# Attention with sinks: the sink logit as one more column of the scores, written by a product of the identity

## The reference, cut to what matters

```python
s_win = jnp.where(ok, s_win, NEG)
s_sink = jnp.broadcast_to(sink.reshape(1, 1, G, R, 1, 1), s_ctx.shape[:-1] + (1,))
w = jax.nn.softmax(jnp.concatenate([s_win, s_ctx, s_sink], axis=-1), axis=-1)
o = einsum(w[..., :K3], vw) + einsum(w[..., K3:K3 + L], v_c)
```

## Time and profile before

| what | value |
| --- | --- |
| median of 3 runs | 1803.98 us (1803.07 to 1807.21) |
| the profiled execution | 1804.19 us, of which the span shown in the profile is 1802.2 us |
| granted TensorE clock, mean | 0.983 of full speed |
| group B of layer 0, first maximum | at 357.4 us from the start of the span |
| group B of layer 1, last maximum | at 1355.2 us |

### The profile page before, as it was taken

The page is one execution under the profiler, slowest core; times in us unless marked ns, Lnnn a source line. Parts: engine busy times, 40 slices in busy tenths (PEclk is TensorE's granted clock), DMA queues, the critical chain, the costliest instruction groups (busy, mean ns, idle before and its releaser), DMA issues. The chain is left out here.

```text
span 1802.2 us, 28988 instructions
## 1 busy us (share of the span) xinstructions
PE 1681.4 (93%) x11814; PEld 1489.5 (83%) x11814; DVE 1176.8 (65%) x1676; ACT 823.4 (46%) x1244; POOL 271.1 (15%) x212
## 2 busy tenths in 40 slices
PE   6999999989898999999999989899898989999998
PEld 4778897768778999899999869769677778989897
DVE  5374737677348797886987965653767484747472
ACT  5433326646227534535435463232655283527161
POOL 0243632301200000000000023362311200000000
PEclk9999999999999999999999999999999999999999
DMA  9541112200346348258276023122300355546251
GB/s 384 167 155 56 51 48 91 86 1 2 139 149 270 132 175 315 95 207 317 70 283 241 23 101 131 71 84 99 135 2 1 117 195 226 202 149 249 102 187 47
DMA packets 45456, 250.27 MB, mean 139 GB/s; under 512 B 5998, under 2 KB 7452, under 8 KB 26652
## 3 DMA queue, kind: packets, MB, share of 16 engines
q1 hardware_dynamic: 43420, 245.49, 36.9%
q10 hardware_dynamic: 1920, 3.15, 0.5%
HBM read 218.73 MB, written 26.74 MB: 136 GB/s over the span
## 5 line engine op out<-in xcount | busy, mean ns | idle before, releaser
L880 POOL TENSOR_TENSOR w_lo<-raw,w_hi 128x512 fp32r<-128x512 f32 x124 | 176.2, 1453 | 959.5 <-ACT w_hi L1017 937.1
L3473 PE MATMUL ps<-op_hi,w_hi 128*128 128x384 f32 x880 | 301.2, 342 | 20.5 <-DVE xT L2636 9.5
L3473 PE MATMUL ps<-op_lo,w_hi 128*128 128x384 f32 x880 | 298.0, 339 | 0.0
L3473 PE MATMUL ps<-op_hi,w_lo 128*128 128x384 f32 x880 | 298.0, 339 | 0.0
L1534 ACT ACTIVATE w_hi<-raw 128x1024 fp32r<-128x1024 f32 x96 | 101.4, 1058 | 200.3 <-PE ps L3473 140.1
L3473 PEld LDWEIGHTS ps<-op_hi,w_hi 128*128 128x128 f32 x880 | 167.3, 190 | 28.5 <-issue 16.8
L3473 PEld LDWEIGHTS ps<-op_lo,w_hi 128*128 128x128 f32 x880 | 167.5, 190 | 0.0
L3473 PEld LDWEIGHTS ps<-op_hi,w_lo 128*128 128x128 f32 x880 | 167.2, 190 | 0.0
L1470 ACT ACTIVATE w_hi<-raw 128x1024 fp32r<-128x1024 f32 x80 | 82.3, 1053 | 143.7 <-PE ps L3436 123.7
L3144 PE MATMUL ps<-w_hi,h_hi 128*128 128x256 f32 x448 | 131.2, 293 | 0.0
L2590 DVE TENSOR_TENSOR w_lo<-raw,w_hi 128x1024 fp32r<-128x1024 f32 x96 | 116.0, 1218 | 20.2 <-ACT w_hi L1534 20.0
(11 more groups left out here) (406 smaller groups left out, 3947.6 us busy)
## 6 DMA issues: line engine op xcount, KB each, us to landing
raw<-w_big SPq DMA_DIRECT2D x96, 1024.0 KB, 6.2
raw_m<-w_modl SPq DMA_DIRECT2D x21, 1024.0 KB, 5.8
op_hi<-op_cache SPq DMA_DIRECT2D x21, 768.0 KB, 4.7
op_lo<-op_cache SPq DMA_DIRECT2D x21, 768.0 KB, 6.3
raw<-w_modl SPq DMA_DIRECT2D x14, 1024.0 KB, 4.9
op_hi<-op_cache SPq DMA_DIRECT2D x21, 512.0 KB, 4.0
op_lo<-op_cache SPq DMA_DIRECT2D x21, 512.0 KB, 5.6
first_mod<-w_modl SPq DMA_DIRECT2D x8, 1024.0 KB, 21.0
```

The lines of the kernel that those rows point to most:

```text
L880: ins = nc.gpsimd.tensor_tensor(w_lo[r][:, ks, :], src[:, ks, :], w_hi[r][:, ks, :].bitcast(F32), ALU.subtract)
L3473: ins = mm(bank(base + g, 0, h), wide(w)[:, k, g * P:(g + 1) * P], ops[hl][:, k, 0:h], start=(p in FRESH and k == 0 and q == 0), stop=(k = ...
```

## The change

The sink becomes a real column of the scores. Behind the 256 context scores, in column 256 of banks 1 and 3, `scores` writes the sink with a product of the float32 identity and the sink's column of `rowc`, once for each head, for pairs of group B. Head a's stands before L3099, head b's between L3106 and L3109. `score_width` makes the maximum and the exponential one column wider for `m == 1`, so the exponential's row sum holds the sink's part, and the transposes don't read that column. The minimum, `se`, its exponential, the addition to the denominators, their semaphore and their tiles go, and `maxima` is the same single reduction for both groups.

```diff
--- before.py
+++ after.py
@@ -173,14 +173,10 @@
     csw = keep("csw", [KD, 32])
     wg = keep("wg", [2, P])
     rowc = keep("rowc", [4 + 2 * 256])
-    nsink = keep("nsink", [4])
     eps = keep("eps", [1])
-    mx = keep("mx", [2, 2])
     nb = keep("nb", [2, 2])
     gqk = keep("gqk", [4])
     gqk_swap = keep("gqk_swap", [4])
-    se = keep("se", [2, 4])
-    es = keep("es", [2, 4])
     psum_e = keep("psum_e", [2, 4])
     dex = keep("dex", [2, TILES])
     mp = keep("mp", [TILES])
@@ -416,6 +412,10 @@
     def pairs_to(l):
 
         return sum(len(att_pairs(i)) for i in range(l + 1))
+
+    def score_width(m, lo):
+
+        return T - lo + m
 
     def key_span(m, j):
 
@@ -1300,7 +1300,7 @@
                 lo, _, _ = key_span(m, j)
                 jp = u // 2 % 2
                 act.wait_ge(*((sem("nba_ready"), a0 + u + 1), (sem("nbb_ready"), b0 + u + 1))[hb])
-                nc.scalar.activation(prob_of(u)[:, hb, 0:T - lo], bank(2 * hb, lo, T - lo), ACT.Exp,
+                nc.scalar.activation(prob_of(u)[:, hb, 0:score_width(m, lo)], bank(2 * hb, lo, score_width(m, lo)), ACT.Exp,
                                      bias=nb[:, u % 2, hb:hb + 1], scale=1.0,
                                      accum_out=psum_e[:, jp, 2 * p + hb:2 * p + hb + 1]).then_inc(sem("exp_done"), 1)
 
@@ -1367,9 +1367,6 @@
                     if u:
                         probs(l, u, 0, a0, b0)
                         probs(l, u, 1, a0, b0)
-                    if m == 1 and p == 1:
-                        nc.scalar.activation(es[:, u // 2 % 2, :], se[:, u // 2 % 2, :],
-                                             ACT.Exp).then_inc(sem("es_ready"), 1)
                     if u >= 1:
                         evac(u - 1)
                     if GATE_U <= u < GATE_U + 3:
@@ -1871,16 +1868,8 @@
                 dve.wait_ge(*((sem("sca_done"), sa0 + u + 1), (sem("scb_done"), sb0 + u + 1))[hb])
                 if u >= 2:
                     dve.wait_ge(sem("exp_done"), e0 + 2 * u - 2)
-                if m == 0:
-                    v.tensor_reduce(nb[:, u % 2, hb:hb + 1], bank(2 * hb, lo, T - lo), AX_X, ALU.max,
-                                    negate=True).then_inc(ready, 1)
-                else:
-                    step(v.tensor_reduce(mx[:, u % 2, hb:hb + 1], bank(2 * hb, lo, T - lo), AX_X, ALU.max,
-                                         negate=True))
-                    step(v.tensor_tensor(nb[:, u % 2, hb:hb + 1], mx[:, u % 2, hb:hb + 1], nsink[:, h:h + 1],
-                                         ALU.min))
-                    v.tensor_tensor(se[:, u // 2 % 2, 2 * p + hb:2 * p + hb + 1], nb[:, u % 2, hb:hb + 1], rowc[:, h:h + 1],
-                                    ALU.add).then_inc(ready, 1)
+                v.tensor_reduce(nb[:, u % 2, hb:hb + 1], bank(2 * hb, lo, score_width(m, lo)), AX_X, ALU.max,
+                                negate=True).then_inc(ready, 1)
 
             def in_proj(l):
                 pending = None
@@ -2143,7 +2132,6 @@
                 s4 = lvec(l, LV_GSW, 4)
                 v.tensor_scalar(gqk_swap[:, 0:4:2], s4[:, 0:4:2], HD ** -0.5, None, ALU.mult)
                 step(v.tensor_copy(gqk_swap[:, 1:4:2], s4[:, 1:4:2]))
-                v.tensor_scalar(nsink[:], rowc[:, 0:4], -1.0, None, ALU.mult)
 
             def turned(l, i):
                 if i == 0:
@@ -2188,12 +2176,8 @@
 
                 def sums(jj):
 
-                    m, _, _ = pairs[2 * jj]
                     jp = jj % 2
                     dve.wait_ge(sem("exp_done"), e0 + 4 * jj + 4)
-                    if m == 1:
-                        dve.wait_ge(sem("es_ready"), T_("es").add())
-                        step(v.tensor_tensor(psum_e[:, jp, :], psum_e[:, jp, :], es[:, jp, :], ALU.add))
                     v.reciprocal(rs[:, jp], psum_e[:, jp, :]).then_inc(sem("rs_ready"), 1)
 
                 def tile_out(jj):
@@ -3096,6 +3080,8 @@
                                skip_group_check=True)
                 elif u >= 1:
                     pe.wait_ge(sem("exp_done"), e0 + 2 * u - 1)
+                if m == 1:
+                    mm(bank(1, CTX, 1), ident, rowc[:, p:p + 1], start=True, stop=True)
                 ins_a = mm(bank(1, 0, CTX), qf[ra, cols(j)], kf[ra, SEQ:T], start=True, stop=True)
                 if u >= 1 and not masks:
                     pe.wait_ge(sem("exp_done"), e0 + 2 * u)
@@ -3106,6 +3092,8 @@
                     ins_a = mm(bank(0, lo, 512 - lo), qf[ra, cols(j)], kf[ra, k0:k0 + 512 - lo],
                                start=not masks, stop=True, skip_group_check=bool(masks))
                 ins_a.then_inc(sem("sca_done"), 1)
+                if m == 1:
+                    mm(bank(3, CTX, 1), ident, rowc[:, p + 2:p + 3], start=True, stop=True)
                 mm(bank(3, 0, CTX), qf[rb, cols(j)], kf[rb, SEQ:T], start=True, stop=True).then_inc(
                     sem("scb_done"), 1)
```

## The result

The changed kernel takes 1816.78 us (median of 5 runs, 1813.75 to 1817.94) against 1803.98 (5 runs) for the kernel before: a ratio of 1.0065, 95% interval [1.005, 1.008], or 12.8 us more. I had predicted 1810.0 and a range of 1801 to 1814. The sign is right, the size is not, and the range does not hold it. The profiled execution took 1817.43 us with a span of 1815.6 and a granted clock of 0.982.

The account below looks back on a forecast made before the run. The exponential chain bound middle window pairs, with 18.8 us of TensorE waits; the change adds 23.6 us to TensorE over 20 pairs and leaves 1.6 of waits: +6.4, so 1804.19 + 6 = 1810 us, range 1801 to 1814.

Parts of the forecast that it names:

- The two products: Window pairs, TensorE: each added product of the identity with the sink column costs 0.25 us, twice a pair.
- The lost overlap and the turns: Head b's 128-row product stops its scores running beside head a's, 0.43 us a pair; switching between 64 and 128 rows, 0.25.
- The shorter chain: Two steps behind each maximum go; a middle pair's loop through the exponentials gets 0.67 us shorter, 4.92 to 4.50 with one product.
- Waits left: Of TensorE's 18.8 us of waits around the 20 window pairs, 1.6 remain, bounds 0 and 18.8.
- TensorE now sets the pace: Middle window pairs: the bound moves from the exponentials to TensorE, making such a pair 0.3 to 0.7 us longer than 4.92.
- the two loops: TensorE's own work in a middle pair and the next one with denominators: 4.00 to 5.18 and 4.43 to 5.61 us.
- So 1804.19 (the profiled execution; span 1802.2) + 6 = 1810: Whole kernel: the 20 window pairs' loss, +6.4 us, added to the profiled time, with nothing behind the last pair covering it.
- I price them at nothing: Removed small exponentials, additions and negated sinks lie beside TensorE's transposes and values: worth 0, or some 3 us if uncovered.
- my rivals: Products hide, faster (0.10); both cancel (0.30); slower by more than +9 (0.04); steps stay on the chain (no chance given).
- More than that: Rival: 1.33 us a window pair, loads hindered on both products and turns in full, +9.3, so 1813.5; chance 0.04.
- Its remark on edge pairs: An edge pair's second maximum comes 0.9 us behind the first, its column being late, where the reduction only takes 0.6.

Follow-up runs that it names:

- The chain alone: Changed kernel without its two sink products and the extra column, so the sink is left out: 1802.06 us with moved addresses, 1796.82 with addresses of before.
- the first experiment: Changed kernel with four unused tiles kept where the removed ones lay, so every tile has its address of before: 1807.84 us, ratio 1.0012.
- the third: Changed kernel with 128 bytes left free in front of the large tiles only, small tiles staying moved: 1807.42 us, ratio 1.0008.

## Why the prediction was wrong

- **The two products** (0.25 each): right. Head a's takes 0.26, and from head b's first pass to L3097's 0.31, its turn and load included.
- **The lost overlap and the turns** (0.43 and 0.25): right in sum. 0.93 from L3092 to the values against 0.25 + 0.43 + 0.25; 0.94 in an edge pair. Counted as in the prediction, TensorE's work rose by 5.0 + 18.8 - 2.8 = 21.0 us and not by 23.6, though. In a pair of context queries, which has no latent scores, it rose by 0.98 (from the first score product to the values 0.80 before, 1.78 from the head a product on after); four of these make up 0.8 of the missing 2.6. The rest isn't traced. The shares of overlap and turns were not measured apart.
- **The shorter chain** (the exponential 0.92 after the maximum, the second 0.79 behind it): 0.92 and 0.88. The chain alone gave -10.2 where I had -10.7. In these pairs the exponentials aren't the bound any more, so the 0.09 costs nothing.
- **Waits left** (1.6): 2.8, mis-sized. That and the 21.0 (which is worked out from the +5.0, and no measurement of its own) are why the stages show +5.0 and not +6.4. "TensorE now sets the pace" held: L3079 waits for an exponential 3 times, where L3095 did 17 times, and the two loops worked out as 5.18 and 5.61 take 5.09 and 5.41.
- **"So 1804.19 (the profiled execution; span 1802.2) + 6 = 1810"**: this is the step that failed. It lets everything outside the 20 pairs stand as before. I priced every instruction that went ("The four-element exponential and addition of each of the ten tiles, and the negated sink of each layer, lie beside TensorE's transposes and values; I price them at nothing", and the chain alone at -9.9 to -10.2 for -10.7 bears that out), but never the bytes that their tiles took. In its place the runs show a term for the place of the large tiles: +8.2 us at equal clock for the kernel before with only the addresses changed (ratio 1.005), and +4.0 for the changed kernel with its addresses kept (ratio 1.0012), so about 7 to 9 us of the 12.8. None of my rivals held that. What the window pairs lost would by itself have given 1804.2 + 5.0 = 1809.
- The raw medians alone would leave a gap: with old addresses the changed kernel's stages are 5.0 longer, and it measures 1.6 (interval 0.2 to 4.2) longer. Most of that gap is the clock: the mean over its executions is 0.983, that of the kernel before beside it 0.981. At equal clock it is +4.0, and +4.7 with only the large tiles kept. By what mechanism an address changes the spacing of the passes stays open.

Of the rivals, "More than that" came nearest in its number (1813.5), and by luck. It needed 1.33 us a pair, and the pairs took 21.0 / 20 = 1.05. Its remark on edge pairs was right (the second maximum starts 0.93 behind the first, 1362.44 - 1361.51, where the reduction takes 0.69), but TensorE doesn't wait for it: it is busy for all 40.72 us of layer 1's stage.

## What to carry to other kernels

A change that removes or adds a small tile moves every tile behind it: keep the addresses with a filler when you measure an edit, and try a few offsets of the large matmul operands as a change of its own. A small product of 128 rows between the 64-row matmuls of two heads, which would else run side by side, costs several times itself (0.93 us against 0.25 here); give it the rows of the head that it belongs to. Compare kernels at an equal granted clock, or over many executions, when the difference is some tenths of a per cent. A shorter dependent chain is worth the waits that it ends only as long as what replaces it doesn't land on the engine that waited.

## What was not expected of the hardware

- The spacing of matmul passes depends on where the large tiles lie: 173.2 to 173.3 or 176.7 ns for 384 float32 columns, in stretches of one kind or the other; offsets 256 bytes apart behaved alike.
- TensorE's granted clock fell to 0.50 (1.2 GHz instead of 2.4) at about 22 us from the start in every profiled execution but one, for a time that doesn't go with the kernel: in the kernel before it is back at 1.00 from 26 us, in the changed one from 32. With the large tiles moved by +128 it is short and by +384 long; in the first experiment short and in the third long. The long one makes an execution some 2 us longer: the first and third experiment, alike up to there but for the place of small tiles, start their first mask at 354.7 and 356.8. The one in the changed kernel's layer 0 made its stage 54.0 and not 52.4 (columns as above):

```profile
399.00:400.00 1.00, 1.00 (x10) 0.67 (x10) 0.89 (x2) 0.48 (x1) 0.00 (x0) 0.80 0.00 0
400.00:401.00 1.00, 1.00 (x12) 0.87 (x10) 0.36 (x1) 1.00 (x3) 0.00 (x0) 0.50 0.00 0
...
403.00:404.00 1.00, 1.00 (x11) 0.95 (x10) 0.93 (x2) 0.49 (x1) 0.00 (x0) 0.99 0.00 0
```

TensorE was busy all through these microseconds, and in the 14 us before them its one stop was 0.56 us. Why the clock fell there, no row shows.
